# First delta-rule turn of a two-layer block: units in another order, and the beta rows multiplied on GpSimd

## What is computed

```python
proj = u @ w_in
qkv = jax.nn.silu(causal_dwconv(proj[..., :GDN_QKV_DIM], conv_w))
z = proj[..., GDN_QKV_DIM:GDN_QKV_DIM + GDN_VAL_DIM]...
beta = jax.nn.sigmoid(b)
g = -jnp.exp(a_log) * jax.nn.softplus(a + dt_bias)
gc = jnp.cumsum(g, axis=-1)
decay = jnp.exp(jnp.where(incl, gc[..., :, None] - gc[..., None, :], -jnp.inf))
m = jnp.where(strict, beta[..., :, None] * kk * decay, 0.0)
a = m + jnp.eye(C)
sol = lax.linalg.triangular_solve(a, rhs, lower=True, unit_diagonal=True)
...
o = rms_norm(o, norm_gain) * jax.nn.silu(z)
```

## Time and profile before

| what | number |
|---|---|
| median of 3 runs | 1759.01 us (1757.73 to 1761.03) |
| the profiled execution's own time | 1760.05 us |
| its span | 1758.2 us |
| busy in the span: PE, DVE, ACT, POOL | 1727.1, 1410.0, 1022.0, 85.5 us |
| stage of turn 0 | about 323 to 376 us |

### The profile page before, as it was taken

The page is one execution under the profiler, slowest core; times in us unless marked ns, Lnnn a source line. Parts: engine busy times, 40 slices in busy tenths (PEclk is TensorE's granted clock), DMA queues, the critical chain, the costliest instruction groups (busy, mean ns, idle before and its releaser), DMA issues.

```text
span 1758.2 us, 32341 instructions
## 1 busy us (share of the span) xinstructions
PE 1727.1 (98%) x12926; PEld 1544.2 (88%) x12926; DVE 1410.0 (80%) x2409; ACT 1022.0 (58%) x1720; POOL 85.5 (5%) x163
## 2 busy tenths in 40 slices
PE   7999999999999999999999999999999999999998
PEld 6888888888988988889888888888898889988887
DVE  4748879798886598888989886988989898777664
ACT  3647764667876677655655413655556555475553
POOL 0000001000000000010101000010101010000000
PEclk9999999999999999999999999999999999999999
DMA  5246559443432466577888743788968786536552
GB/s 199 84 186 207 188 175 358 153 151 129 137 110 98 144 214 203 189 275 268 313 285 301 275 145 127 294 297 287 333 248 306 282 321 242 177 127 202 189 191 96
DMA packets 102819, 373.90 MB, mean 213 GB/s; under 512 B 11440, under 2 KB 11600, under 8 KB 102544
## 3 DMA queue, kind: packets, MB, share of 16 engines
q1 hardware_dynamic: 80352, 289.77, 46.8%
q0 software_dynamic: 22320, 82.09, 13.6%
HBM read 370.74 MB, written 1.08 MB: 211 GB/s over the span
## 4 chain that ended last, share of the span: by engine, by line
PE 87%; DVE 7%; ACT 3%; issue 2%; DMA 1%; DVEq 0%; SPq 0%; ACTq 0%
PE ps L650 37%; PE ps L653 20%; PE ps L657 3%; PE ps L658 3%; PE ps L659 3%; PE ps L1074 2%; PE ps L748 2%; DVE weights_lo L618 2%; PE ps L1259 1%; PE ps L2381 1%; ACT weights_hi L611 1%; DVE arena L2500 1%; PE ps L2407 1%; DMA ffn_tiles<-in_ada 1%; PE ps L1451 1%
## 5 line engine op out<-in xcount | busy, mean ns | idle before, releaser
L618 DVE TENSOR_TENSOR weights_lo<-weight_ring,weights_hi 128x1024 fp32r<-128x1024 f32 x493 | 601.1, 1221 | 125.6 <-ACT weights_hi L611 125.1
L611 ACT ACTIVATE weights_hi<-weight_ring 128x1024 fp32r<-128x1024 f32 x493 | 518.0, 1057 | 162.2 <-PE ps L650 106.9
L650 PE MATMUL ps<-u_halves,weights_hi 128*128 128x512 f32 x2048 | 495.0, 391 | 1.0 <-DVE u_halves L473 0.5
L650 PEld LDWEIGHTS ps<-u_halves,weights_hi 128*128 128x128 f32 x2048 | 376.3, 188 | 75.8 <-DVE weights_lo L618 1.0
L653 PEld LDWEIGHTS ps<-u_halves,weights_lo 128*128 128x128 f32 x2048 | 266.0, 191 | 10.5 <-DVE weights_lo L618 0.3
L653 PE MATMUL ps<-u_halves,weights_lo 128*128 128x256 f32 x2048 | 274.2, 283 | 0.2
L650 PE MATMUL ps<-act_halves,weights_hi 128*128 128x512 f32 x952 | 231.3, 391 | 0.0
L650 PEld LDWEIGHTS ps<-act_halves,weights_hi 128*128 128x128 f32 x952 | 173.5, 188 | 32.4
L887 DVE SCALAR_TENSOR_TENSOR ffn_tiles<-ffn_tiles,cond 128x1024 f32<-128x1024 f32 x144 | 175.3, 1219 | 4.1 <-DMA ffn_tiles<-in_ada 4.0
L780 ACT ACTIVATE ffn_tiles<-ps 128x512 f32<-128x512 f32 x128 | 76.0, 594 | 143.5 <-PE ps L653 143.3
L653 PEld LDWEIGHTS ps<-act_halves,weights_lo 128*128 128x128 f32 x1088 | 142.3, 191 | 7.3 <-DVE weights_lo L618 0.9
(11 more groups left out here) (347 smaller groups left out, 2338.5 us busy)
## 6 DMA issues: line engine op xcount, KB each, us to landing
weight_ring<-in_w SPq DMA_DIRECT2D x545, 512.0 KB, 4.0
ffn_tiles<-in_ada POOLq DMA_DIRECT2D x144, 512.0 KB, 5.1
scaled<-gates_scratch POOLq DMA_DIRECT2D x8, 512.0 KB, 6.0
arena<-in_alibi POOLq DMA_DIRECT2D x1, 1536.0 KB, 6.8
h<-in_x SPq DMA_DIRECT2D x4, 256.0 KB, 4.3
out<-u SPq DMA_DIRECT2D x4, 256.0 KB, 2.1
consts<-in_consts SPq DMA_DIRECT2D x1, 592.0 KB, 9.8
cond<-in_cond SPq DMA_DIRECT2D x1, 512.0 KB, 10.8
```

What stands on the lines that cost most here:

```text
L611: nc.scalar.activation(w_slot(s)[0], ring[:, n % RING], ACT.Copy).then_inc(hi_ready, 1)
L618: nc.vector.tensor_tensor(lo, ring[:, n % RING], hi.bitcast(F32), ALU.subtract).then_inc(lo_ready, 1)
L650: return nc.tensor.matmul(ps[:, bank], hi, halves, start=start, stop=stop, skip_group_check=True)
```

## The change

For turn 0, z unit 8 is made third, z unit 9 between units 5 and 6, z unit 10 between 7 and 11; the weights come in this order (`FIRST_TURN`). The gates' sigmoid becomes exp, ln and exp, in the table set that is loaded at that point, and the running sum is made before the multiplication by the head's factor. The split of the third unit goes into a fourth slot that is not yet in use otherwise. In every turn POOL multiplies the beta rows by the strict mask (two instructions, one for each half) and by the row decays (one); DVE's table becomes one multiplication. In turn 0 only the first of the masked products stays ahead of level 0; the others (`masked_second_dve`) follow DVE's mask of level 0.

```diff
+FIRST_TURN = (0, 1, 8, 2, 3, 4, 5, 9, 6, 7, 10, 11)
...
+                if 2 <= gdn_in and gdn_out < 0:
+                    s = 3 if gdn_in == 2 else gdn_in % GDN_SPLIT
...
         def level_first_pe(pe, i, lv):
...
-                    if t == 0:
+                    if i == 0 and t == 1:
+                        pe.wait_ge(g_masked, 1)
+                    if i and t == 0:
                         pe.wait_ge(g_masked, 2 * i + 2)
                 else:
+                    if lv == SMALL and t == 0:
+                        pe.wait_ge(g_masked, 2 * i + 2)
...
         def gdn_pe(pe):
...
+            gdn_unit_pe(pe, 0, 1)
+            gdn_unit_pe(pe, 0, 8)
+            gdn_unit_pe(pe, 0, 2)
+            gdn_unit_pe(pe, 0, 3)
+            gate_cols_pe(pe)
             gdn_unit_pe(pe, 0, 4)
-            gate_cols_pe(pe)
             gdn_unit_pe(pe, 0, 5)
             qk_sums_pe(pe, 0)
+            gdn_unit_pe(pe, 0, 9)
             gdn_unit_pe(pe, 0, 6)
+            kk_pe(pe, 0)
             gdn_unit_pe(pe, 0, 7)
-            kk_pe(pe, 0)
-            gdn_unit_pe(pe, 0, 8)
-            gdn_unit_pe(pe, 0, 9)
+            gdn_unit_pe(pe, 0, 10)
             v_turn_pe(pe, 0)
-            gdn_unit_pe(pe, 0, 10)
             gdn_unit_pe(pe, 0, 11)
...
         def m_table_dve(dve, steps, i):
-            dve.wait_ge(g_tabs, 2 * i + 2)
-            m, w = steps.mark, steps.wait
-            rows = b_row.rearrange("p n (t s) -> p t n s", t=2)
-            m(nc.vector.tensor_tensor(ber, egr, b_row[:, :, P:T], ALU.mult))
-            m(nc.vector.tensor_tensor(m_tab, qk_tab, rows, ALU.mult))
-            w()
-            strict = const("strict_up").unsqueeze(1).to_broadcast([P, 2 * GB, P])
-            tab = m_tab.rearrange("p t n s -> p (t n) s")
-            nc.vector.tensor_tensor(tab, tab, strict, ALU.mult).then_inc(g_mtab, 1)
+            dve.wait_ge(g_tabs, 2 * i + 1)
+            dve.wait_ge(g_brow, 2 * i + 2)
+            nc.vector.tensor_tensor(m_tab, qk_tab, m_tab, ALU.mult).then_inc(g_mtab, 1)
...
         def gdn_turn_dve(dve, steps, i):
             level_dve(dve, i, 0)
+            if i == 0:
+                masked_second_dve(dve, steps, 0)
+                turn_blocks_dve(dve, i, 0)
             decay_args_dve(dve, steps, n, 0)
             decay_args_dve(dve, steps, n, 1)
-            turn_blocks_dve(dve, i, 0)
+            if i:
+                turn_blocks_dve(dve, i, 0)
...
         def gdn_pool(pool):
...
+            strict = const("strict_up").unsqueeze(1).to_broadcast([P, GB, P])
             for i in range(N_TURNS):
                 if i:
-                    pool.wait_ge(g_mtab, i)
+                    pool.wait_ge(g_ber, i)
+                    pool.wait_ge(g_brow, 2 * i)
                     pool.wait_ge(g_tabs, 2 * i)
                 for n, dst in ((1, g_row), (0, b_row)):
                     pool.dma_start(dst, gates_dram[n][GB * i:GB * i + GB, :].partition_broadcast(P)).then_inc(g_rows, 16)
+                pool.wait_ge(g_rows, 32 * (i + 1))
+                if i:
+                    pool.wait_ge(g_mt, 2 * i)
+                for t in range(2):
+                    nc.gpsimd.tensor_tensor(m_tab[:, t], b_row[:, :, t * P:(t + 1) * P], strict, ALU.mult).then_inc(g_brow, 1)
+                pool.wait_ge(g_tabs, 2 * i + 2)
+                nc.gpsimd.tensor_tensor(ber, egr, b_row[:, :, P:T], ALU.mult).then_inc(g_ber, 1)
```

More of the change, by code:

```diff
@@ L1398, in flat, with gdn_at @@
             return x.rearrange("p a b -> p (a b)")
+        def gdn_at(i, j):
+            return 12 * i + j if i else FIRST_TURN.index(j)
         def blocks_until(i, lv, t):
@@ L1406, in lower_until, with level_bank @@
             return 2 * (LEVELS - SMALL) * i + 2 * (lv - SMALL) + t + 1
-        def level_bank(lv, which, t):
+        def level_bank(i, lv, which, t):
             if lv < SMALL:
-                return {"p": 4, "xi": 6}[which] + t
+                return {"p": 4 if i else 2, "xi": 6}[which] + t
             a = 4 + 2 * (lv % 2)
@@ L1525, in level_first_pe @@
                         pe.wait_ge(g_xt, lower_until(i, lv - 1, 0))
-                bank = level_bank(lv, "p", t)
+                bank = level_bank(i, lv, "p", t)
                 for n in range(GB):
@@ L1553, in level_second_pe @@
                 if lv < LEVELS - 1:
-                    bank = level_bank(lv, "xi", t)
+                    bank = level_bank(i, lv, "xi", t)
                     for n in range(GB):
@@ L1570, in level_second_pe @@
                         pe.wait_ge(g_xt, lower_until(i, lv - 1, 1))
-                bank = level_bank(lv, "ix", t)
+                bank = level_bank(i, lv, "ix", t)
                 for n in range(GB):
@@ L1747, in gdn_gates_act, with gdn_softplus_end_act, gdn_beta_ln_act, gdn_beta_act @@
             m(nc.scalar.activation(nea[a], cols[a, COL["a_log"]:COL["a_log"] + 1], ACT.Exp))
-            w()
+        def gdn_softplus_end_act(act, steps):
+            steps.wait()
+            a = slice(32, 48)
             nc.scalar.activation(ta[a], ta[a], ACT.Ln, bias=cols[a, COL["one"]:COL["one"] + 1]).then_inc(g_soft, 1)
-        def gdn_beta_act(act):
-            nc.scalar.activation(gates[0:16], ps[0:16, 4, 0:T], ACT.Sigmoid).then_inc(g_beta, 1)
+            steps.mark(nc.scalar.activation(tb_[0:16], ps[0:16, 4, 0:T], ACT.Exp, scale=-1.0))
+        def gdn_beta_ln_act(act, steps):
+            steps.wait()
+            steps.mark(nc.scalar.activation(tb_[0:16], tb_[0:16], ACT.Ln, bias=cols[0:16, COL["one"]:COL["one"] + 1]))
+        def gdn_beta_act(act, steps):
+            steps.wait()
+            nc.scalar.activation(gates[0:16], tb_[0:16], ACT.Exp, scale=-1.0).then_inc(g_beta, 1)
         def gdn_hi_act(act, i, j):
@@ L1771, in tap_act @@
             w = COL["gdn_conv"] + 32 * i + 4 * j + 3
-            nc.scalar.activation(cbuf[:, x % 4], ps[:, (12 * i + j) % 2, 0:T], ACT.Identity, scale=cols[:, w:w + 1]).then_inc(g_tap, 1)
+            nc.scalar.activation(cbuf[:, x % 4], ps[:, gdn_at(i, j) % 2, 0:T], ACT.Identity, scale=cols[:, w:w + 1]).then_inc(g_tap, 1)
         def silu_conv_act(act, i, j):
@@ L2144, in masked_products_dve, with masked_second_dve @@
             nc.vector.tensor_tensor(pair(qkb[:, i % 2]), qk1, pair(qk_tab[:, 1]), ALU.mult).then_inc(g_masked, 1)
+        def masked_second_dve(dve, steps, i):
+            pair = lambda x: x.rearrange("p (m b) s -> p m b s", m=2)
             qk0 = ps[:, 4:6, T:T + P].unsqueeze(2).to_broadcast([P, 2, 2, P])
@@ L2208, in gdn_dve @@
             gdn_clear_dve(dve)
+            split_lo(dve, "gdn_in", 2)
             taps_conv_dve(dve, steps, 0, 0)
-            split_lo(dve, "gdn_in", 2)
+            gdn_lo_dve(dve, 0, 0)
             taps_conv_dve(dve, steps, 0, 1)
-            gdn_lo_dve(dve, 0, 0)
+            gdn_lo_dve(dve, 0, 1)
             gates_dve(dve, steps)
-            gdn_lo_dve(dve, 0, 1)
-            for j in range(2, 5):
-                taps_conv_dve(dve, steps, 0, j)
-                gdn_lo_dve(dve, 0, j)
+            gdn_lo_dve(dve, 0, 2)
+            taps_conv_dve(dve, steps, 0, 2)
+            gdn_lo_dve(dve, 0, 3)
+            taps_conv_dve(dve, steps, 0, 3)
+            gdn_lo_dve(dve, 0, 4)
+            taps_conv_dve(dve, steps, 0, 4)
+            gdn_lo_dve(dve, 0, 5)
             gate_cols_dve(dve, steps)
@@ L2967, in weight_stream @@
     for i in range(GH // GB):
-        units += [tiles[t] for t in gdn_turn_tiles(i)] + [tiles[32 + 4 * i + j] for j in range(4)]
+        turn = [tiles[t] for t in gdn_turn_tiles(i)] + [tiles[32 + 4 * i + j] for j in range(4)]
+        units += turn if i else [turn[j] for j in FIRST_TURN]
     units += gdn_out_units(x["gdn_w_out"][0])
```

96 lines of the change are left out of this document (50 added, 46 removed).

## The result

The changed kernel takes 1763.45 us (median of 14 runs, 1760.19 to 1768.43), the kernel before 1759.83 us (14 runs, 1757.62 to 1762.36). The ratio is 1.0021, with a 95% interval of 1.0014 to 1.0029: slower by 3.6 us, where a gain of 2 us was forecast, 1757.0 in a range of 1753.5 to 1761.5.

The account below looks back on a forecast made before the run. PE, busy 1727.1 of 1758.2 us, bounds the kernel, but DVE sets turn 0's end. A gain of 2.0 us, other parts nothing, gives 1758.0 from the profiled 1760.05, or 1757.0 from the 1759.0 median; range 1753.5 to 1761.5.

Parts of the forecast that it names:

- PE's list, 367.1: Turn 0: with z units between, PE's list runs through and reaches level 0 at 367.1 instead of 374.17, 7 us earlier.
- DVE sets the end, 2.0 us won: Turn 0, levels 0 and 1: DVE's queue behind unit 7's convolution limits the gain to 1.6 to 2.2 us, taken as 2.0.
- Rival 1: Level 0 of turn 0: DVE finishes the matrix by PE's 367.1, the full 7 us are won, 1752 us; chance 0.21.
- The second wait that was computed: Level 1 of turn 0: PE waits for DVE ahead of L1559, over 1 us.
- Whether DVE slows down while POOL multiplies: DVE beside POOL's multiplications: no slowdown, priced at nothing; other end a full stop of DVE for two masks of 1.5 us.
- Rival 2: Around 367 us: POOL's masks of turn 1 stop DVE, which loses 1.1 to 3 us; 1758.4 to 1760.5 us, chance 0.23.
- POOL's loads for the next turn: Row loads, now behind POOL's multiplications and ahead of DVE's table: they start earlier, not later; priced at nothing.
- From there on turns are as before: Behind level 1 of turn 0: later turns unchanged, everything shifts as a whole, no further gain or loss.
- Rival 3: Ahead of POOL's first multiplication: an ISA instruction may fetch code, 13 to 15 us free, 1767 us at 24; chance 0.10.
- Gates, the fourth slot, the order of the weights: Gates lie beside PE's first units, under 1 us uncovered; split slot and weight order cause no load wait; priced at nothing.

Follow-up runs that it names:

- the order alone: Kernel before with the new order of turn 0 and early gates; DVE keeps all three multiplications, row loads stay behind its table: 1757.10 us, ratio 0.9984.
- late masks: Changed kernel, but GpSimd begins a next turn's masks only after both masks of level 1 of this turn: 1760.64 us, ratio 1.0000 to the kernel before.
- GpSimd alone: Kernel before with only the changed `m_table_dve`, `gdn_pool` and the wait for `g_ber`, old order kept: 1767.49 us, ratio 1.0044.
- GpSimd alone and the loads put back: Kernel before with GpSimd's multiplications, row loads of the next turn waiting for DVE's table: 1761.33 us, ratio 1.0006 to the kernel before.

## Why the prediction was wrong, by its steps

- **PE's list, 367.1:** right: PE comes to level 0 at 367.53.
- **DVE sets the end, 2.0 us won:** right, for the order alone. Its stage is 1.9 us shorter than before, its ratio 0.9984, and putting the masked products back takes all of it. Rival 1, the whole 7 us, did not come: PE waited 2.75 us at level 0, where 2.5 were computed. The second wait that was computed, over 1 us ahead of level 1's second product, did not come: there PE, at the lower clock, was the later one, by up to 0.4 us.
- **"Whether DVE slows down while POOL multiplies ... nothing is the one end and the one I take":** this step failed first. A group of pair masks that meets two masks of POOL takes 3.10 to 3.14 instead of 1.17 us, in turns 0, 1 and 2; the decay arguments of turn 0 take 3.65 instead of 2.15. Its row, DVE beside a memset, was of the wrong kind: beside memsets in the masks' place the pair masks keep their 1.17 us. The mechanism was Rival 2, which named the place too, near 367, and gave it a loss of 1.1 to 3 us; in turn 0 it was 1.93. The Trainium skill's rule that the prediction set against the row (page "SBUF — State Buffer", section "SBUF: two separate sides") agrees with the traces: DVE instructions with two SBUF inputs got longer beside GpSimd's multiplications, the convolution with one did not (1.51 us), and nothing got longer beside memsets, which only write. A mask took 1.3 us where nothing held it up (2.59 for two), within the prediction's bounds of 0.5 to 1.5; in the changed kernel's turn 1 two took 3.01.
- **"POOL's loads for the next turn ... start earlier than before, not later", priced at nothing:** this step failed too. It saw the move and asked only whether rows come in time. At their new time, 388.84 and 448.62 instead of 406.48 and 464.50, 1 MB of rows comes shortly ahead of the levels' short matmuls, and PE's instructions come late. Put back, the kernel takes 1760.28 us, which is Rival 2's case (1758.4 to 1760.5). With either repair alone the time lies within the range (1760.28 with the loads back, 1760.64 with late masks); it takes both losses to leave it.
- **"From there on turns are as before":** wrong by both. The row that it went by, ends at 432 us, and behind that PE of the kernel before had a gap of 0.90 us itself, at 504.36. In the first trace level 0 of turn 1 starts 1.28 us late (433.86 against 432.58), of which 0.56 is the first gap; turn 1 adds the gap of 1.63 and 16 matmuls at 1.2 GHz behind it (1.5 us); in turn 2 PE waits 0.73 us for a weight split, because pair masks beside POOL's masks (3.13 us) lie ahead of it on DVE again.
- **Rival 3:** not seen. POOL's first multiplication starts when its rows have landed (7.75 us of idle, ended by the DMA); the two masks are done at 351.45, and DVE's table begins at 358.7.
- **Gates, the fourth slot, the order of the weights:** nothing in the traces speaks against their price of nothing; they were not tried by themselves.

In ratios, taken step by step from the order alone to the changed kernel, the parts are: the order -0.16%, the masks beside the pair masks +0.16%, the row loads +0.15%, what remains of POOL's part (the decay arguments of turn 0, a longer split where the late masks lie) +0.06%, which no interval here can tell from zero: together +0.21%, as steps of one chain must add up. Each of the middle terms is uncertain by 0.1 to 0.15%. By the other way, through late masks, they are 0.21% for the masks and 0.10% for the loads.

The order alone beats both kernels: 1757.10 us, 3.1 us less than before on the same chip. That this comes within 0.1 us of the forecast is in part luck: the gain is 3.1 us where 2.0 were forecast, and its trace shows 1.9 in the stage.

## What to carry to other kernels

Where DVE sets the end, work given to GpSimd is not off the path if it reads SBUF while DVE works on two SBUF operands: in this case each overlapped multiplication of 1.3 us cost DVE 0.95 us in the pair masks. Beside the convolution, which reads one operand from PSUM, it cost nothing. To price such a pair, look for a row of the same kind (what it reads, not how large it is); a row of another kind is no bound. Of a transfer that a change moves, ask not only whether its data come in time, but what runs while it moves and what else has to be loaded for that, instructions too.

## What the runs showed that was not expected

PE's waits without a releaser are part of every version: before has one of 0.90 us at 504.36, the order alone 0.89 at 503.05. The changed kernel has none there, in either trace, just after DVE made PE wait 0.73 us. That goes through all traces: the five in which PE waits 0.72 or 0.73 us for that weight split have no gap there, the nine others have one of 0.6 to 0.9 us. So a wait can absorb a gap that would have come anyway.

The same wait need not cost the same. Behind the 2.12 us ahead of unit 3 the granted clock from 341 to 346 us is 0.68 in the kernel before and 0.66 with GpSimd alone, but 1.00 with GpSimd alone and the loads put back, whose wait is 2.12 us too:

```profile
341.52 0.39 PE L657 MATMUL ps<-u_halves,weights_hi 128*128 128x256 f32 x1 [2.12 <-DVE u L2061]
341.74 0.28 PE L658 MATMUL ps<-u_halves,weights_hi 128*128 128x256 f32 x1
```

By the matmuls that ran at the lower level in the kernel before (15 at 0.094 us more each), that is about 1.4 us of difference between two executions, as much as a gap. Why the clock did not fall in the third stays open.
